# Two subtractions moved ahead of two additions on VectorE, in each of four feed-forward layers

## The reference

```python
for i in range(DEPTH):                          # 4
    y = rmsnorm(h, norm_mix_g[i])
    y = ...                                     # pool, attention, conv, pool
    h = h + y
    h = h + swiglu_ffn(rmsnorm(h, norm_ffn_g[i]), ffn_w_gate[i], ffn_w_up[i], ffn_w_down[i])
return rmsnorm(h[:, N_META:], final_norm_g)

def swiglu_ffn(h, w_gate, w_up, w_down):        # hidden width 2816 = 22 blocks of 128
    return (jax.nn.silu(h @ w_gate) * (h @ w_up)) @ w_down
```

## Time and profile before

| | us |
|---|---|
| median of three runs | 2163.19 |
| the profiled execution | 2163.19 |
| its span, first to last instruction | 2161.4 |
| TensorE busy | 2042.5 (95%) |
| VectorE busy | 1668.6 (77%) |
| ScalarE busy | 827.7 (38%) |
| GpSimd busy | 263.2 (12%) |
| TensorE on the chain that ended last | 76% of the span |
| VectorE on it | 9% of the span |

### The profile page before, as it was taken

How to read it: one execution, slowest core, us unless ns; L and a number is a source line. 1 busy time by engine, 2 the same in 40 slices (tenths; PEclk the granted TensorE clock), 3 DMA queues, 4 the chain that set the end, 5 groups by cost and what they waited for, 6 DMA issues and landing times.

```text
span 2161.4 us, 40083 instructions
## 1 busy us (share of the span) xinstructions
PE 2042.5 (95%) x15690; PEld 1971.6 (91%) x15690; DVE 1668.6 (77%) x2356; ACT 827.7 (38%) x1240; POOL 263.2 (12%) x351
## 2 busy tenths in 40 slices
PE   5699999999998899999999999999999958999997
PEld 5699999998887799999999999999999956899996
DVE  6887888767776479777969996588787778977794
ACT  3243343334443234333446443343443323433341
POOL 4200000322122410000040000200000151000003
PEclk8899999999997999999999999999999988999999
DMA  3323442332121133333341120224423322333332
GB/s 105 109 79 98 116 116 77 90 109 60 49 58 49 40 91 86 98 97 97 95 121 40 39 59 20 79 79 118 116 84 92 87 60 69 96 100 97 97 95 91
DMA packets 306394, 181.49 MB, mean 84 GB/s; under 512 B 6556, under 2 KB 303517, under 8 KB 306278
## 3 DMA queue, kind: packets, MB, share of 16 engines
q1 hardware_dynamic: 304702, 175.01, 28.2%
q10 hardware_dynamic: 1048, 2.71, 0.3%
q0 software_dynamic: 528, 2.16, 0.3%
HBM read 177.74 MB, written 4.81 MB: 84 GB/s over the span
## 4 chain that ended last, share of the span: by engine, by line
PE 76%; DVE 9%; DVEq 6%; issue 5%; POOLq 2%; ACT 1%; DMA 0%; POOL 0%; SPq 0%; ACTq 0%
PE ps L757 39%; PE ps L963 32%; DVEq L2300 3%; DVE cv L2301 1%; DVE pool_s L1788 1%; PE ps L1098 1%; PE ps L779 1%; PE ps L1122 1%; POOLq L662 1%; DVE pooled L1799 1%; DVE w_lo L1687 1%; POOLq L659 1%; DVEq L2285 0%; DVE h L1809 0%; PE ps L787 0%
## 5 line engine op out<-in xcount | busy, mean ns | idle before, releaser
L757 PE MATMUL ps<-y_hi,w_hi 128*128 128x264 f32 (+1 forms) x1152 | 259.5, 302 | 67.6 <-DVE w_lo L1687 50.7
L963 PE MATMUL ps<-t_lo,y_hi 128*128 128x264 f32 (+1 forms) x1008 | 285.9, 284 | 0.0
L963 PE MATMUL ps<-t_lo,w_hi 128*128 128x264 f32 (+1 forms) x1008 | 285.9, 284 | 0.0
L963 PE MATMUL ps<-t_hi,w_lo 128*128 128x264 f32 (+1 forms) x1008 | 285.3, 283 | 0.0
L963 PE MATMUL ps<-t_hi,y_lo 128*128 128x264 f32 (+1 forms) x1008 | 285.3, 283 | 0.0
L963 PE MATMUL ps<-t_hi,w_hi 128*128 128x264 f32 (+1 forms) x1008 | 285.0, 283 | 0.1
L963 PE MATMUL ps<-t_hi,y_hi 128*128 128x264 f32 (+1 forms) x1008 | 284.9, 283 | 0.0
L757 PE MATMUL ps<-hid_hi,w_hi 128*128 128x264 f32 (+1 forms) x1232 | 284.5, 300 | 0.4 <-DVE hid_lo L1983 0.4
L757 PE MATMUL ps<-hid_lo,w_hi 128*128 128x264 f32 (+1 forms) x1232 | 283.8, 301 | 0.0
L757 PE MATMUL ps<-hid_hi,w_lo 128*128 128x264 f32 (+1 forms) x1232 | 283.0, 299 | 0.0
L757 PEld LDWEIGHTS ps<-y_hi,w_hi 128*128 128x128 f32 x1152 | 184.3, 192 | 80.3 <-issue 64.9
(11 more groups left out here) (272 smaller groups left out, 4295.2 us busy)
## 6 DMA issues: line engine op xcount, KB each, us to landing
w_raw<-in_ffn_w_gate SPq DMA_DIRECT2D x88, 512.0 KB, 5.1
w_raw<-in_ffn_w_up SPq DMA_DIRECT2D x88, 512.0 KB, 4.7
w_raw<-in_ffn_w_down SPq DMA_DIRECT2D x64, 512.0 KB, 4.3
w_raw<-in_ffn_w_down SPq DMA_DIRECT2D x32, 384.0 KB, 4.3
w_raw<-in_attn_w_qkv SPq DMA_DIRECT2D x16, 512.0 KB, 3.9
w_raw<-in_conv_w_in SPq DMA_DIRECT2D x16, 512.0 KB, 4.2
w_raw<-in_attn_w_qkv SPq DMA_DIRECT2D x16, 256.0 KB, 2.9
w_raw<-in_attn_w_o SPq DMA_DIRECT2D x8, 512.0 KB, 3.8
```

The source lines that it names most:

```text
L757: mm = pe.matmul(ps[:, bank + hf, 0:half], w[:, slot, col:col + P], x(hf), start=begin and w is m.w_hi and n == 0, stop=end and w is m.w_lo)
L963: mm = pe.matmul(ps[:, bank, 0:hw], w[:, at:at + P], b[:, t, k, 0:hw], start=k == 0 and n == 0, stop=k == 3 and n == 2)
```

## The change

In the first `part(0, 0)` of each layer the last two calls of `factor_lo` stood behind the first two additions; they now stand ahead of them. Nothing else changes: the instructions, their operands and their semaphores are the same, and so is the order on the four other engines.

```diff
@@ part(i, j) @@
                     add_part(i, j, 0)
                     add_part(i, j, 1)
-                    if j == 0:
-                        factor_lo(3, T3, 2, x_blocks(True, hw))
-                        factor_lo(4, T4, 2, x_blocks(False, hw))
                     prepare(i, 2 * j, "gate")
                     add_part(i, j, 2)
                     operands_lo(i, 2 * j, "gate", 2)
@@ ffn @@
                 factors_second()
                 for c in (2, 3):
                     split_lo(part0 + c, 0, 0, SLOT)
+                factor_lo(3, T3, 2, x_blocks(True, hw))
+                factor_lo(4, T4, 2, x_blocks(False, hw))
                 part(0, 0)
```

## The result

The changed kernel takes 2186.87 us in the median (2186.84 to 2188.08), the kernel before 2162.94 us (2161.96 to 2164.79) in the same rounds: a ratio of 1.0111, with a 95% interval of 1.0094 to 1.0129. The forecast was 2183.8 us, slower, range 2177 to 2188. The profiled execution took 2187.3 us with a span of 2185.5 us, 24.1 us more than before.

A forecast was written before the change was run, and what follows sets the result against it. TensorE alone was taken to set the end. Stalls of 15.4 us (12.0 in layers 0 to 2, 3.4 in layer 3) plus 5.2 us for the clock made 20.6 us, so 2183.8 us, range 2177 to 2188.

The forecast's parts named there:

- Step 1: First part of layer 0, VectorE: both t_hi are there when the moved subtractions start, the first with 0.18 us to spare.
- Step 2: Block 4 in layer 0: TensorE stands still until the delayed first addition ends, 4.0 us.
- Step 3: Block 6 and the products in layer 0: no second stall, as the second addition ends at 142.05, needed at 146.75.
- Steps 4 and 5: Layer 0 returns nothing; layers 0 to 2 cost 12.0 us; layer 3 costs 3.4 us after two small waits go.
- Step 6: TensorE's clock falls to 1.2 GHz after the new stalls: 1.3 us each, 5.2 us for four.
- rival B: The clock stays low longer after each of the four stalls, as in attention, 4.6 us each: 2197.0 us; chance 0.09.
- A: The stalls come at block 4, but the clock does not fall or only hidden in the stall: 2178.6 us; chance 0.17.
- C: TensorE does not stand at block 4, as it could go on or the additions don't release it: 2163.2 us; chance 0.04.
- D: Faster: VectorE closes its idle gap between the additions and starts operands 0.8 us earlier per layer: 2160.0 us; chance 0.02.

The follow-up runs named there:

- filled kernel: The changed kernel with 34 additional matmuls of 240 columns on TensorE ahead of block 3 of the first part in each layer; 2178.77 us, ratio 1.0070.

## Why the prediction was right, point by point

**Step 1 (the subtractions can start early)** held. They ran at 134.90 and 137.17 without idle time. The second t_hi ended at 134.63 + 1.96 = 136.59, in time.

**Step 2 (the stall)** had the right mechanism and nearly the right size: block 4 was forecast 4.0 us late in three layers and 4.16 in the last, and is 4.13, 4.13, 4.14 and 4.25 late. The room of 0.56 us, one matmul's start against one addition's end, carried the forecast, and the subtractions between the additions, which cost nothing, show that it is the first addition that matters. The estimate of 0.05 us from the addition's end to TensorE was too small: in layer 0 it is 140.84 - (139.44 + 1.25) = 0.15 us.

**Step 3 (no second stall)** held: no other new wait is in the trace. The third addition waits 3.21 us for TensorE in layer 0 where it had waited for nothing.

**Steps 4 and 5 (nothing returned but layer 3's two waits)** held, with wrong prices for the two waits. The 0.5 us in the earlier trace rows is a wait of the weight load, and the earlier trace rows has no idle time ahead of that matmul; without it TensorE's first product comes 0.16 us earlier (the subtractions between the additions). The 0.42 us at 1911.21 returned 0.60. In all, the stalls with what came back make 16.2 us in the trace (23.1 us of the networks less 7.0 for the clock), where 15.4 were forecast, and 15.9 in the trace of the filled kernel.

**Step 6 (the clock)** had the right mechanism and too small a size. I took 1.3 us for each stall, 5.2 in all, hoping that one in four might be free; all four dropped the clock, three for 1.4 to 1.5 us, and layer 0 for 2.5 us, since its slow stretch was 6.8 us long with 5.5 us of it behind the stall. That is 7.0 us by the table. The reading under it was incomplete: the trace of before has more than four gaps of 2 us and over that TensorE entered at the full clock. One ends at 1798.93 (2.22 us, then 3.4 us at the low level), and one is as long as the new stalls and was followed by 10.2 us:

```profile
722.49 1.19 PE L1139 MATMUL ps<-square,ones 128*128 128x512 f32 x1 [4.03 <-POOL square L719]
```

Both speak for a fall at every stall, and the second, in attention as well, for the long ones of rival B.

The trace is 24.1 us longer where 20.6 were forecast. Of the missing 3.5 us, 0.76 are in the stalls, 1.76 in the clock behind them, and 0.98 in stretches that the change doesn't touch and that the forecast had at nothing. The measured time lies only 1.1 us under the upper end of the range, and the last of these three could as well have come out larger: it is the length of slow stretches behind gaps that were there before. From the convolution to layer 2's x_low the trace is 1.23 us longer, and there the low level lasts 16 x 2 x 0.43 = 13.7 us against 12 x 2 x 0.43 = 10.3 before. The window of before comes first, then that of the changed kernel:

```profile
1314.00:1326.00 12.00, 12.00 (x59) 11.73 (x58) 6.66 (x22) 3.61 (x4) 0.00 (x0) 0.57 0.29 87
```

```profile
1323.00:1339.00 16.00, 16.00 (x82) 15.75 (x81) 9.34 (x26) 5.70 (x7) 0.00 (x0) 0.57 0.24 67
```

The other stretches have the same sign: ahead of layer 3's x_low 34.2 us against 30.7 (0.47 us longer), in attention 30.7 against 34.1 (0.50 us shorter). In the filled kernel the gap that ends at 1388.29 dropped no clock, and that stretch is 1.74 us shorter. Why such a stretch comes out longer in one trace than in another no run here shows.

The Trainium skill, TensorE: Matmul & The Clock Gate, section Terms, counts half of the throttled time as lost. In layer 0 there are 5.52 us at the low level behind the stall: by that rule 2.76 us, by the measured distances 2.47. Block 4 to the first product takes 155.06 - 140.84 = 14.22 us there, and 11.75 us in the kernel with one subtraction ahead, which has the same passage behind a stall at the full clock (138.46 to 150.21). The difference is 2.47 us, so the distances are the better measure.

**The rivals.** A (no fall of the clock) is what the filled kernel makes true, at 2178.8 us where 2178.6 was worked out, in part by chance as said above. B (the clock low for far longer, 10.3 us for each stall) didn't come; 6.8 us was the longest. C (TensorE wouldn't stand) and D (faster, from VectorE's earlier start) are refuted: the four gaps of TensorE answer C, and the move between the additions gives VectorE its 0.8 us and gains nothing that can be told from no change.

## What to carry to other kernels

When work is moved on an engine that isn't the bound, compare two rooms: the time from the end of what stands behind it to the first instruction that needs that, and the same for the work itself. Here the additions had 0.56 us and the subtractions 5.7 us. A swap of 4.5 us between them cost the difference and the 0.15 us from the addition to TensorE, in full, since TensorE had no waits behind it in three of the four layers that could return it. And a stall of the matmul engine is to be priced with its clock: the five stalls of 4 us cost 1.4 to 2.6 us on top. The four of 1.7 to 1.9 us cost nothing of that kind, but that isn't a safe length: in the same trace a gap of 1.78 us, ending at 1807.25, was followed by 3.4 us at the low level.

## What the runs showed of the hardware that I had not expected

A gap of the same length doesn't always do the same to TensorE's clock. The convolution's gap of 3.6 us left it at 2.4 GHz in four of the ten traces and dropped it to 1.2 GHz in six, for 3.4 us in five and 6.8 in one. The gap of 4.1 us ahead of L768 in layer 3, the same in all ten, was followed by 3.4 us at the low level in five traces, 6.8 in four and 10.2 in one. The low stretch can lie partly in the idle time, where it costs nothing, and four stalls of 8.8 us left about as much slow time behind them as four of 4.1 (15.8 against 15.6 us). In an execution's time all this shows only where TensorE sets the end.
